# A decoder layer with 32 experts on one core: first stage, state products, output norm and first bias rearranged

## Chip, cores and metric

The kernel runs on one core of a Trainium2 chip. What is measured is device time in microseconds, the median of several runs of one program. Everything is float32. The engines are PE (TensorE, matrix products; PEld is its weight load), DVE (VectorE), ACT (ScalarE), POOL (GpSimd), SP (SyncE, which here only issues transfers) and the DMA engines. Each of the five runs its own list of instructions in order; they wait for each other by semaphores.

## The reference, cut

```python
xn = rmsnorm(h, norm1_gain[l]);  proj = xn @ w_in[l]            # h: 16 meta + 256 tokens, 1024 wide
u, q, fpre, v, og, gates = jnp.split(proj, IN_SPLITS, axis=-1)
# s5_mixer: 32 groups of 16 channels and 64 complex states each
lam_bar = jnp.exp(lam * dt)                                     # dt = exp(log_dt), one per group
b_bar = ((lam_bar - 1.0) / lam)[:, :, None] * b_mat
bu = jnp.einsum('gph,blgh->blgp', b_bar, u32)
_, states = lax.associative_scan(combine, (a, bu), axis=1)      # s_t = lam_bar * s_(t-1) + bu_t
y = jnp.real(jnp.einsum('ghp,blgp->blgh', c_mat, states)) + d_skip * u32
y = jax.nn.gelu(y);  y_s5 = y * jax.nn.sigmoid(y @ w_glu)
# hgrn2_mixer: 4 heads of 128, gated linear recurrence in chunks
o = o * lax.rsqrt(jnp.mean(o * o, axis=-1, keepdims=True) + EPS)   # the output norm, per head
y_hg = o.reshape(bsz, seq_len, HG_WIDTH) * gn_gain * jax.nn.silu(g)
merged = gate_s5 * (y_s5 @ w_branch_s5[l]) + gate_hg * (y_hg @ w_branch_hgrn[l])
h = h + merged @ w_out[l]
h = h + moe(rmsnorm(h, norm2_gain[l]), ...)   # top 4 of 32 experts: gate_up, clamped SwiGLU, down
y = rmsnorm(h, final_norm_gain)[:, N_META:]
```

The token count is 272 (16 meta tokens and 256 tokens), and only the 256 are given back. Each of the 32 experts has 8 MB of gate_up weights and 4 MB of down weights, so the expert stage reads 403 MB.

## The kernel before

**Opening.** SP loads x in two halves (xload0, xload1), the first group of w_in, then B, C and the second group of w_in. ACT's queue loads log_dt, the identity, the first gain, the eigenvalues of S5 (s5rows, three transfers into s5r and small) and the constants; POOL's queue loads the meta tokens and the small gain rows (prow, grow). DVE sums the squares of both halves (L1107), ACT takes the roots (after an Exp of log_dt, L455), DVE scales both halves (L1112), PE turns them to channels-by-tokens (L681) and DVE and ACT lay them out with the gain as xnT (L1126, L466). `keep_warm` is a run of products on ones whose result nobody reads.

**Projections.** xnT times w_in gives 36 tiles, the list PROJ: each is one bank of PSUM, made by eight products (sixteen instructions) of PE, and copied out by ACT (`next_proj`, semaphores proj and proj_free; two banks alternate). `project(n)` on PE makes the next n of the list. The first four tiles are u. Windows of w_in alternate between two places, and a window is loaded when the one before the last is used up.

**S5 constants.** DVE works out lam_bar and the factor of B on s5r, 16 partitions by 128 columns (L1120 to L1162), with Sin and Exp from ACT (L469 to L472). PE turns four rows of it (L760), DVE copies them to s5c on 128 partitions (L1167). Then the B products on DVE (L1173 to L1185), turned by PE (b_turned), laid out (b_laid), and the first product with u, `bu(0)` (L772), which also waits for the fourth tile's copy (L771).

**S5 loop.** 16 steps on DVE (L1213), each for 128 states: four products with sine and cosine, two sums, two scans, and six products back. ACT makes the sines (`turns_of`, `sines_of`), POOL moves u for the imaginary half. PE has eight rounds: LOOP_TILES says how many projection tiles stand ahead of and behind each round's `bu(p + 1)` (L780 to L785), and every second round sums the outputs (`y_of`). ACT's list of copies follows the same numbers (L526 to L554).

**HGRN2.** Seven levels (`level(n)`, PE products of 64 columns, with DVE on both sides), the glu of S5 and the other projection tiles are laid between each other by hand (L820 to L842). Behind level(5) come the state products (L836 to L840), for each of four heads one with 16 rows (the meta chunk, khTm) and one with 128 rows (khT). Then the last tiles, the outputs o (o_mm), and the branches: `branch(br, b)` makes two tiles of 256 columns of y @ w_branch. Between them stands the output norm of HGRN2: ACT squares o (o2, L592), PE sums by eight products with one column of ones (ms_mm, L871), ACT takes the root of 8 columns, DVE the reciprocal and spreads it on diagonals (dgs, L1373), PE spreads these by ones (inv_mm, L878), and DVE multiplies (yh, L1378). SP waits for inv_mm and for eight branch tiles ahead of loading pieces 3 and 4 (L359).

**Experts.** After w_out, the second norm, the router and the choice, 32 items run, one for each expert. An item's weights are six pieces of 2 MB; ten places hold pieces, and from piece 10 on SP loads piece r when r - 9 pieces are used (piece_used, L380). The first ten are loaded behind o_mm, og_used, br_mm and wo_mm (L354 to L378). An item adds the bias by four products of one-hot rows (ohb, bgu; L1021), runs four gate_up pieces, adds the item before to the sum, gathers the next item's rows, turns h, and runs two down pieces (L1006 to L1060). Ahead of item 0 the rows are gathered on PE (gather_part), copied by ACT, turned (`turn_gathered(0, 7)`, L1003) and laid by DVE. Four `keep_warm` products stand ahead of that turn (L947).

## Time and profile before

| | us |
|---|---|
| median of 3 runs (1188.56 to 1191.16) | 1188.78 |
| the profiled execution | 1189.03 |
| its span | 1187.2 |
| PE busy in it | 1152.6 |
| DVE, ACT busy | 441.7, 181.3 |

The profile's page counts 434.27 MB read from HBM, 367 GB/s over the span. The granted clock of PE has a mean of 0.994 of full speed (2.4 GHz). A row of the timeline or of a stage can cover many instructions (the x at its end); a busy PE is one that has work in flight, which is not the same as PE at its peak. An idle time in brackets says how long the engine stood before the instruction and which instruction released it.

### The profile page before, as it was taken

What the parts mean: (1) busy time and instruction counts of PE and PEld (TensorE: products, weight loads), DVE (VectorE), ACT (ScalarE), POOL (GpSimd) and SP (SyncE); (2) the same over time, 40 slices, a digit from 0 to 9 for tenths busy, and PEclk for the clock granted to TensorE, in tenths of its full rate; (3) what the DMA queues carried; (4) which work ended last, traced back from release to release, by engine and by line L of the source; (5) the groups of instructions that cost most, each with busy time, mean ns of one, the idle gap of its engine ahead of it and who ended that gap; (6) DMA issues with size and microseconds to landing.
All of it is one profiled execution on the core that took longest, in us unless ns stands there. A gap on an engine that the chain in (4) does not pass through costs nothing.

```text
span 1187.2 us, 13854 instructions
## 1 busy us (share of the span) xinstructions
PE 1152.6 (97%) x5506; PEld 501.7 (42%) x5506; DVE 441.7 (37%) x1105; ACT 181.3 (15%) x330; POOL 7.7 (1%) x19
## 2 busy tenths in 40 slices
PE   8999999999999999999999999999999999999996
PEld 7757798763333333333333333333333333333332
DVE  6889983344222222222323332222222222222224
ACT  4545732020000000000000000000000000000001
POOL 1000000000000000000000000000000000000000
...
GB/s 227 187 182 185 130 1 187 387 190 396 415 429 428 426 435 430 429 436 427 432 432 432 429 433 432 431 433 432 433 427 434 432 432 428 435 432 428 433 423 157
DMA packets 46166, 436.42 MB, mean 368 GB/s; under 512 B 17311, under 2 KB 17503, under 8 KB 30257
## 3 DMA queue, kind: packets, MB, share of 16 engines
...
q14 instruction: 10, 0.07, 0.0%
HBM read 434.27 MB, written 1.05 MB: 367 GB/s over the span
## 4 chain that ended last, share of the span: by engine, by line
PE 75%; DMA 20%; DVE 3%; ACT 1%; issue 1%; ACTq 0%; SPq 0%; DVEq 0%
PE ps L661 71%; DMA ring<-in_w_gate_up 16%; PE ps L664 4%; DMA mixed<-in_w_gate_up 3%; DVE ring L1087 1%; ACT ring L440 1%; DMA ring<-in_s_lambda_im 0%; ACT L440 0%; DVE ring L1090 0%; DVE mixed L1093 0%; DVE ring L1260 0%; DVE ring L1093 0%; ACT mixed L440 0%; DVE x L1087 0%; ACT small L440 0%
## 5 line engine op out<-in xcount | busy, mean ns | idle before, releaser
L661 PE MATMUL ps<-ring,mixed 128*64 128x512 f32 (+1 forms) x2560 | 572.0, 589 | 11.9 <-DMA ring<-in_w_gate_up 10.4
L661 PEld LDWEIGHTS ps<-ring,mixed 128*64 128x64 f32 (+1 forms) x2560 | 187.8, 139 | 356.0 <-issue 329.9
L1090 DVE TENSOR_SCALAR mixed<-ps 128x256 f32<-128x256 f32 x128 | 45.4, 417 | 585.8 <-PE ps L661 585.8
L661 PE MATMUL ps<-ring 128*128 128x256 f32 (+7 forms) x936 | 192.5, 395 | 2.5 <-DVE ring L1087 1.8
L661 PEld LDWEIGHTS ps<-ring 128*128 128x128 f32 (+2 forms) x936 | 143.9, 187 | 48.0 <-issue 26.3
L661 PE MATMUL ps<-mixed,cst 128*64 128x512 f32 (+2 forms) x776 | 160.4, 611 | 2.1 <-issue 2.1
L661 PE MATMUL ps<-mixed 128*64 128x512 f32 (+2 forms) x704 | 153.9, 561 | 2.5 <-DMA mixed<-in_w_gate_up 2.3
L440 ACT ACTIVATE mixed<-mixed 128x512 f32<-128x512 f32 (+1 forms) x36 | 24.0, 676 | 485.2 <-DVE mixed L1090 485.2
L661 PEld LDWEIGHTS ps<-mixed 128*64 128x64 f32 (+1 forms) x704 | 57.8, 144 | 87.6 <-issue 80.3
L661 PEld LDWEIGHTS ps<-mixed,cst 128*64 128x64 f32 (+2 forms) x776 | 44.9, 151 | 110.5 <-issue 110.3
L1087 DVE TENSOR_TENSOR x<-ps,x 128x512 f32<-128x512 f32 (+1 forms) x137 | 84.6, 677 | 15.1 <-PE ps L661 15.1
L440 ACT ACTIVATE mixed<-ps 128x512 f32<-128x512 f32 (+1 forms) x87 | 47.9, 553 | 269.2 <-PE ps L661 215.7
L1087 DVE TENSOR_TENSOR ring<-ring 128x256 f32<-128x256 f32 (+5 forms) x182 | 76.4, 474 | 6.6 <-PE ps L661 3.7
L664 PEld LDWEIGHTS ps<-cst,mixed 128*128 128x128 f32 x256 | 35.9, 210 | 33.5 <-DVE mixed L1087 26.2
L664 PE MATMUL ps<-cst,mixed 128*128 128x128 f32 x256 | 47.9, 310 | 1.6 <-DVE mixed L1087 1.1
L1090 DVE TENSOR_SCALAR cst<-cst,rout 128x64 f32<-128x64 f32 x192 | 44.4, 288 | 1.9 <-issue 1.8
L1562 DVE COPY mixed<-ps 128x512 f32<-128x512 f32 x32 | 22.1, 692 | 50.9 <-PE ps L664 50.9
L440 ACT ACTIVATE cst<-ps 128x256 f32<-128x256 f32 x33 | 12.7, 384 | 178.5 <-PE ps L664 178.5
L440 ACT ACTIVATE ring<-ring 128x272 f32<-128x272 f32 (+5 forms) x50 | 29.8, 602 | 10.7 <-DVE ring L1087 5.7
L1087 DVE TENSOR_TENSOR ring<-ps,ring 128x272 f32<-128x272 f32 x64 | 23.6, 428 | 3.5 <-PE ps L661 3.3
L1093 DVE SCALAR_TENSOR_TENSOR mixed<-mixed 128x512 f32<-128x512 f32 x32 | 22.2, 692 | 1.1
L1087 DVE TENSOR_TENSOR mixed<-mixed 128x512 f32<-128x512 f32 x32 | 22.1, 692 | 1.1
(145 smaller groups left out, 286.2 us busy)
## 6 DMA issues: line engine op xcount, KB each, us to landing
...
ring<-in_w_gate_up SPq DMA_DIRECT2D x28, 2048.0 KB, 16.4
ring<-in_w_down SPq DMA_DIRECT2D x20, 2048.0 KB, 22.0
...
ring<-in_w_in SPq DMA_DIRECT2D x9, 2048.0 KB, 8.8
mixed<-in_w_down SPq DMA_DIRECT2D x4, 2048.0 KB, 16.4
```

Source lines behind the costliest of these rows:

```text
L440: return nc.scalar.activation(o, i, fn, **k)
L661: return nc.tensor.matmul(o, l, r, start=start, stop=stop, skip_group_check=True)
L664: return nc.tensor.transpose(o, i, ident[0:n, 0:n])
L1087: return V.tensor_tensor(out=o, in0=i0, in1=i1, op=op)
L1090: return V.tensor_scalar(o, i, s1, s2, op0, op1) if op1 is not None else V.tensor_scalar(o, i, s1, None, op0)
L1093: return V.scalar_tensor_tensor(out=o, in0=i0, scalar=sc, in1=i1, op0=op0, op1=op1)
L1562: V.tensor_copy(hT, ps[3][:, :].rearrange("p (a b c) -> p a b c", a=4, b=2)).then_inc(s["hT_ready"], 1)
```

## The change

Five parts. **Opening:** DVE sums the squares of the first half only, ACT those of the second; each root takes mean and epsilon in one instruction, and each half is scaled and turned on its own; all of the layout is DVE's. The first two `keep_warm` runs (6 and 3 products) go, and 2 and 1 products stand behind the two turns. The three S5 rows (real, imaginary, and dt spread to the same shape) are turned ahead of the first projection, and the constants are worked out on 128 partitions by 16 columns (s5w), so no turn stands behind them. fraction(0) moves in among the B products, sines_of(0) ahead of a copy. **Tiles:** three tiles instead of four ahead of bu(0), the wait for proj_free there goes, LOOP_TILES begins with (3, 1) and ends with (2, 0), and three tiles instead of two follow the last y_of; ACT's copies move with them. **State products:** the four of 16 rows first, then the four of 128. **Output norm:** PE multiplies the squares by a full square of ones, so each partition has the sum; ACT takes the root of both 128x512 halves, DVE takes the reciprocals of both and multiplies. The branch tiles are numbered singly: one ahead of the ones products, seven behind. **First bias:** item 0's bias products stand ahead of `turn_gathered(0, 7)`, in the place of the four `keep_warm` products.

```diff
         s5r = at(ringf[0:ST], 2 * PC + 2112, 8, P)
-        s5q = at(ringf[0:ST], 2 * PC + 3136, 3, P)
+        s5w = at(ringf, 2 * PC + 3136, 9, ST)
...
-        xs = at(ringf, H0 + 4096, D)
-        xs2 = at(ringf, H0 + 5120, D)
-        v_parts = xs[:, 0:W5]
+        xsq = [at(ringf, H0 + 4096, D), at(ringf, H0 + 1536, D)]
+        xs = [at(ringf, H0 + 4096, D), at(ringf, H0 + 5120, D)]
+        v_parts = xsq[0][:, 0:W5]
...
-        LOOP_TILES = [(2, 1), (2, 1), (2, 1), (1, 2), (2, 1), (2, 1), (2, 1), (3, 0)]
+        LOOP_TILES = [(3, 1), (2, 1), (2, 1), (1, 2), (2, 1), (2, 1), (2, 1), (2, 0)]
...
-            sp.wait_ge(s["inv_mm"], 1)
+            sp.wait_ge(s["yh_ready"], 2)
             sp.wait_ge(s["br_mm"], 8)
...
-            act.wait_ge(s["s5rows"], 48)
-            f(small[0:ST, 2:4], small[0:ST, 0:2], ACT.Exp).then_inc(s["s5r_exp"], 1)
-            for t in range(TT):
-                root(1 + t, small[:, 4 + t:5 + t])
+            def mean_root(v, n):
+                return f(v, v, ACT.Sqrt, scale=1.0 / D, bias=zero_c[0:n, 2:3])
+
+            nc.scalar.preload_act_table(ACT.Sqrt)
+            act.wait_ge(s["var_in"], 1)
+            mean_root(small[:, 4:5], P).then_inc(s["root_out"], 1)
+            act.wait_ge(s["xload1"], 16)
+            link(f(xsq[1], x[:, 1, :], ACT.Square, accum_out=small[:, 5:6]))
+            mean_root(small[:, 5:6], P).then_inc(s["root_out"], 1)
             act.wait_ge(s["meta"], 16)
             link(f(xmn, xm[:, :], ACT.Square, accum_out=small[0:META, 8:9]))
-            f(small[0:META, 8:9], small[0:META, 8:9], ACT.Sqrt, scale=1.0 / D, bias=zero_c[0:META, 2:3]).then_inc(s["root_out"], 1)
-            act.wait_ge(s["inv_m"], 1)
-            f(xmn, xm[:, :], ACT.Identity, scale=small[0:META, 9:10]).then_inc(s["xm_ready"], 1)
-            act.wait_ge(s["gain1_ready"], 1)
-            act.wait_ge(s["turned_x"], TT)
-            for k in range(4, KD):
-                last = f(xnT[:, k, META + P:TOK], ps[3][:, (k - 4) * P:(k - 3) * P], ACT.Identity, scale=gain1[:, k:k + 1])
-            last.then_inc(s["xnT_ready"], 1)
+            mean_root(small[0:META, 8:9], META).then_inc(s["root_out"], 1)
+            act.wait_ge(s["s5rows"], 48)
+            f(s5r[:, 2, :].rearrange("p (g n) -> p g n", g=2), small[0:ST, 0:2].unsqueeze(2).to_broadcast([ST, 2, 64]), ACT.Exp)\
+                .then_inc(s["s5r_exp"], 1)
+            act.wait_ge(s["s5r_v"], 1)
+            f(s5c[:, 0, :], s5w[:, 3, :], ACT.Exp).then_inc(s["s5r_exp"], 1)
             act.wait_ge(s["s5r_ang"], 1)
-            f(s5r[:, 6, :], s5r[:, 5, :], ACT.Sin, scale=TWO_PI).then_inc(s["s5r_sin"], 1)
-            f(s5r[:, 7, :], s5r[:, 5, :], ACT.Sin, scale=TWO_PI / 2).then_inc(s["s5r_sin"], 1)
-            act.wait_ge(s["s5r_v"], 1)
-            f(s5r[:, 4, :], s5r[:, 2, :], ACT.Exp).then_inc(s["s5r_exp"], 1)
+            f(s5w[:, 6, :], s5c[:, 1, :], ACT.Sin, scale=TWO_PI).then_inc(s["s5r_sin"], 1)
+            f(s5w[:, 7, :], s5c[:, 1, :], ACT.Sin, scale=TWO_PI / 2).then_inc(s["s5r_sin"], 1)
...
-            next_proj(2)
+            next_proj()
             act.wait_ge(s["s5cols_ready"], 1)
             act.wait_ge(s["consts"], 16)
             turns_of(0)
             turns_of(1)
+            sines_of(0)
             next_proj()
-            sines_of(0)
...
             decay_exp(0)
-            next_proj()
+            next_proj(2)
             act.wait_ge(s["gelu_in"], 1)
             f(yt, yt, ACT.Sigmoid, scale=GELU_C).then_inc(s["gelu_sig"], 1)
...
-            act.wait_ge(s["ms_mm"], 1)
-            f(rms[:, 0:8], ps[7][:, 0:8], ACT.Sqrt, scale=1.0 / P, bias=zero_c[:, 2:3]).then_inc(s["rms_out"], 1)
+            for b in range(2):
+                act.wait_ge(s["ms_mm"], b + 1)
+                f(oms[:, 512 * b:512 * b + 512], ps[6 + b][:, :], ACT.Sqrt, scale=1.0 / P, bias=zero_c[:, 2:3])\
+                    .then_inc(s["rms_out"], 1)
...
             tr(ps[6][:, 0:8], grow1[:, :], 8).then_inc(s["gain1_turned"], 1)
-            keep_warm(6, 7)
...
-                    last = tr(ps[2 * t + k // 4][:, (k % 4) * P:(k % 4 + 1) * P], (xs, xs2)[t][:, k * P:(k + 1) * P])
+                    last = tr(ps[2 * t + k // 4][:, (k % 4) * P:(k % 4 + 1) * P], xs[t][:, k * P:(k + 1) * P])
                 last.then_inc(s["turned_x"], 1)
+                keep_warm(2 - t, 7)
             pe.wait_ge(s["xm_ready"], 1)
             for k in range(KD):
                 last = tr(ps[5][:, k * META:(k + 1) * META], xmn[:, k * P:(k + 1) * P], META)
             last.then_inc(s["turned_m"], 1)
+            pe.wait_ge(s["s5rows"], 48)
+            pe.wait_ge(s["s5r_exp"], 1)
+            for j in range(3):
+                last = tr(ps[4][:, j * ST:(j + 1) * ST], s5r[:, j, :], ST)
+            last.then_inc(s["s5rows_turned"], 1)
...
-            keep_warm(3, 7)
...
-            pe.wait_ge(s["xnT_ready"], 2)
+            pe.wait_ge(s["xnT_ready"], 1)
...
             project()
             pe.wait_ge(s["consts"], 16)
-            pe.wait_ge(s["s5r_v"], 2)
-            for j, row in enumerate((4, 5, 2, 3)):
-                last = tr(ps[7][:, j * ST:(j + 1) * ST], s5r[:, row, :], ST)
-            last.then_inc(s["s5rows_turned"], 1)
-            project()
             pe.wait_ge(s["bz_ready"], 1)
             for c in range(2):
                 for t in range(4):
@@ -768,7 +769,6 @@
             last.then_inc(s["b_turned"], 1)
             project()
             pe.wait_ge(s["b_laid"], 1)
-            pe.wait_ge(s["proj_free"], 4)
             bu(0)
             pe.wait_ge(s["s5cols_ready"], 1)
...
             y_of(ST // 4 - 1)
-            project(2)
+            project(3)
...
             for h in range(HEADS):
                 hs = slice(h * P, (h + 1) * P)
                 mm(ps[6][:, hs], khTm[:, hs], v_m[:, hs], h == 0, h == 3)
+            for h in range(HEADS):
+                hs = slice(h * P, (h + 1) * P)
                 last = mm(ps[7][:, hs], khT[:, h, :], v_a[:, 0, hs], h == 0, h == 3)
             last.then_inc(s["st_mm"], 1)
...
             pe.wait_ge(s["o2_ready"], 2)
-            for j in range(8):
-                last = mm(ps[7][:, j:j + 1], o2[:, j * P:(j + 1) * P], ones[:, 0:1], j == 0, j == 7)
-            last.then_inc(s["ms_mm"], 1)
-            branch(0, 1)
-
-            pe.wait_ge(s["diag_ready"], 1)
             for b in range(2):
-                last = mm(ps[6 + b][:, :], ones[:, :], dgs[:, 512 * b:512 * b + 512], True, True)
-            last.then_inc(s["inv_mm"], 1)
-            branch(0, 2)
-            branch(0, 3)
+                mm(ps[6 + b][:, :], ones[:, :], o2[:, 512 * b:512 * b + 512], True, True).then_inc(s["ms_mm"], 1)
+            for m in range(1, KD):
+                branch(0, m)
             pe.wait_ge(s["branchh_w"], 16)
             pe.wait_ge(s["yh_ready"], 2)
-            for b in range(4):
-                branch(1, b)
+            for m in range(KD):
+                branch(1, m)
...
             gather_part(1).then_inc(s["gathered"], 1)
-            keep_warm(4)
...
+            def add_bias(w):
+                pe.wait_ge(s["ohb_ready"], w + 1)
+                for b in range(2):
+                    for h in range(2):
+                        rows = slice(E * (2 * b + h), E * (2 * b + h + 1))
+                        last = mm(ps[b][SLOTS * h:SLOTS * (h + 1), :], ohb[rows, :], bgu[rows, :], True, False)
+                last.then_inc(s["ohb_used"], 1)
+
+            pe.wait_ge(s["expert_rows"], 64)
+            add_bias(0)
             turn_gathered(0, 7)
-            pe.wait_ge(s["expert_rows"], 64)
...
                 pe.wait_ge(s["xg_ready"], w + 1)
-                pe.wait_ge(s["ohb_ready"], w + 1)
-                for b in range(2):
-                    for h in range(2):
-                        rows = slice(E * (2 * b + h), E * (2 * b + h + 1))
-                        last = mm(ps[b][SLOTS * h:SLOTS * (h + 1), :], ohb[rows, :], bgu[rows, :], True, False)
-                last.then_inc(s["ohb_used"], 1)
+                if m > 0:
+                    add_bias(w)
...
-            for t in range(TT):
-                dve.wait_ge(s["xload%d" % t], 16)
-                link(V.tensor_tensor_reduce((xs, xs2)[t], x[:, t, :], x[:, t, :], 1.0, 0.0, MU, AD, small[:, 4 + t:5 + t]))
-                ts(small[:, 4 + t:5 + t], small[:, 4 + t:5 + t], 1.0 / D, EPS, MU, AD).then_inc(s["var_in"], 1)
-            for t in range(TT):
-                dve.wait_ge(s["root_out"], t + 1)
-                link(V.reciprocal(small[:, 6 + t:7 + t], small[:, 4 + t:5 + t]))
-                ts((xs, xs2)[t], x[:, t, :], small[:, 6 + t:7 + t], None, MU).then_inc(s["xs_ready"], 1)
+            def scaled(n, v, inv, dst, src):
+
+                dve.wait_ge(s["root_out"], n)
+                link(V.reciprocal(inv, v))
+                return ts(dst, src, inv, None, MU)
+
+            def lay_turned(t, b):
+                dve.wait_ge(s["turned_x"], t + 1)
+                tt(xnT[:, 4 * b:4 * b + 4, META + t * P:META + (t + 1) * P],
+                   ps[2 * t + b][:, :].rearrange("p (a n) -> p a n", a=4), wide(gain1[:, 4 * b:4 * b + 4], P), MU)
+
+            dve.wait_ge(s["xload0"], 16)
+            V.tensor_tensor_reduce(xsq[0], x[:, 0, :], x[:, 0, :], 1.0, 0.0, MU, AD, small[:, 4:5]).then_inc(s["var_in"], 1)
+            scaled(1, small[:, 4:5], small[:, 6:7], xs[0], x[:, 0, :]).then_inc(s["xs_ready"], 1)
             dve.wait_ge(s["gain1_turned"], 1)
             V.tensor_copy(gain1, ps[6][:, 0:8]).then_inc(s["gain1_ready"], 1)
-            dve.wait_ge(s["root_out"], 3)
-            V.reciprocal(small[0:META, 9:10], small[0:META, 8:9]).then_inc(s["inv_m"], 1)
-            R = lambda j: s5r[:, j, :]
-            R2 = lambda j: s5r[:, j, :].rearrange("p (g n) -> p g n", g=2)
-            dt2 = wide(small[0:ST, 2:4], 64)
-            dve.wait_ge(s["s5r_exp"], 1)
-            tt(R2(2), R2(0), dt2, MU).then_inc(s["s5r_v"], 1)
             dve.wait_ge(s["gain1_ready"], 1)
-            for t in range(TT):
-                dve.wait_ge(s["turned_x"], t + 1)
-                for b in range(2 - t):
-                    tt(xnT[:, 4 * b:4 * b + 4, META + t * P:META + (t + 1) * P],
-                       ps[2 * t + b][:, :].rearrange("p (a n) -> p a n", a=4), wide(gain1[:, 4 * b:4 * b + 4], P), MU)
+            scaled(2, small[:, 5:6], small[:, 7:8], xs[1], x[:, 1, :]).then_inc(s["xs_ready"], 1)
+            lay_turned(0, 0)
+            scaled(3, small[0:META, 8:9], small[0:META, 9:10], xmn, xm).then_inc(s["xm_ready"], 1)
+            lay_turned(0, 1)
+            lay_turned(1, 0)
+            lay_turned(1, 1)
             dve.wait_ge(s["turned_m"], 1)
             tt(xnT[:, :, 0:META], ps[5][:, 0:KD * META].rearrange("p (a n) -> p a n", a=KD), wide(gain1, META), MU)\
                 .then_inc(s["xnT_ready"], 1)
...
+            dve.wait_ge(s["s5rows_turned"], 1)
+            link(V.tensor_copy(s5w[:, 0:3, :], ps[4][:, 0:3 * ST].rearrange("p (a n) -> p a n", a=3)))
+            tt(real, lam_re, dt_c, MU).then_inc(s["s5r_v"], 1)
+            link(tt(angle, lam_im, dt_c, MU))
...
+            link(V.reciprocal(den_c, den_c))
             dve.wait_ge(s["s5r_exp"], 2)
             dve.wait_ge(s["s5r_sin"], 2)
...
+            link(tt(co_im, co_im, angle, SU))
+            tt(co_re, co_re, den_c, MU)
+            tt(co_im, co_im, den_c, MU).then_inc(s["s5cols_ready"], 1)
 
             dve.wait_ge(s["rows_turned"], 1)
...
             link(tt(bb[3], bim, cr, MU))
+            fraction(0)
             tt(bb[0], bb[0], bb[1], SU)
             link(tt(bb[2], bb[2], bb[3], AD))
...
-            fraction(0)
             dve.wait_ge(s["b_turned"], 1)
...
-            link(merge(0, 0))
-            dve.wait_ge(s["rms_out"], 1)
-            link(V.reciprocal(rms[:, 8:16], rms[:, 0:8]))
-            tt(dgs.rearrange("p (a n) -> p a n", a=8), wide(rms[:, 8:16], P), ident.unsqueeze(1).to_broadcast([P, 8, P]), MU)\
-                .then_inc(s["diag_ready"], 1)
+            for b in range(2):
+                root = oms[:, 512 * b:512 * b + 512]
+                dve.wait_ge(s["rms_out"], b + 1)
+                link(V.reciprocal(root, root))
+                tt(yh[:, 2 * b:2 * b + 2, :].rearrange("p a n -> p (a n)"), orn[:, 512 * b:512 * b + 512], root, MU)\
+                    .then_inc(s["yh_ready"], 1)
+            merge(0, 0)
             merge(0, 1)
-            dve.wait_ge(s["inv_mm"], 1)
-            for b in range(2):
-                tt(yh[:, 2 * b:2 * b + 2, :], orn[:, 512 * b:512 * b + 512].rearrange("p (a n) -> p a n", a=2),
-                   ps[6 + b][:, :].rearrange("p (a n) -> p a n", a=2), MU).then_inc(s["yh_ready"], 1)
```

## Rows read from the trace of the kernel before

**Rows 1.** the chain of waits in order of time: start us, us, what
```profile
145.61 95.56 PE ps L661 x468
...
799.26 36.96 DMA ring<-in_w_gate_up
...
1071.01 12.57 PE ps L661 x48
...
1129.31 10.87 PE ps L661 x48
```

**Rows 2.** busy time by stage: us, engines, PEclk, DMA share, GB/s
```profile
core 0: us, PE busy (x) PEld busy (x) DVE busy (x) ACT busy (x) POOL busy (x), PEclk, DMA share, GB/s
800.00:1000.00 200.00, 192.71 (x898) 64.08 (x896) 54.61 (x133) 14.86 (x27) 0.00 (x0) 1.00 1.00 431
```

**Rows 3.** the timeline of SP: start us, us, instruction
```profile
295.34 4.28 SPq L297 DMA_DIRECT2D mixed<-in_w_gate_up  x2
```

**Rows 4.** the same stages view as rows 2, a short stretch of item 0
```profile
294.00:296.00 2.00, 2.00 (x12) 0.54 (x8) 1.89 (x6) 0.30 (x1) 0.00 (x0) 1.00 0.18 74
```

**Rows 5.** DMA issues of the first five microseconds: KB each, us to landing
```profile
ring<-in_w_in SPq DMA_DIRECT2D x1, 2048.0 KB, 12.0
```

**Rows 6.** timeline of the first stage: start us, us, instruction [idle before it, releaser]
```profile
0.98 5.95 PE L661 MATMUL ps<-ones 128*128 128x128 f32 x28 [0.98 <-POOL ones L413]
...
11.10 1.97 PE L664 MATMUL ps<-cst,ring 128*128 128x128 f32 x16 [2.48 <-DVE ring L1090]
...
12.30 2.08 DVE L1087 TENSOR_TENSOR ring<-ps,pcol 128x512 f32<-128x512 f32 x4
...
14.64 3.83 PE L661 MATMUL ps<-ring 128*128 128x272 f32 x16
...
24.41 0.39 PE L664 MATMUL ps<-cst,ring 16*128 16x16 f32 x4 [1.44 <-DVE ring L1087]
...
28.81 1.09 PE L664 MATMUL ps<-cst,ring 128*128 128x128 f32 x8 [0.15 <-DVE ring L1090]
...
34.11 0.74 PE L661 MATMUL ps<-ring 32*128 32x272 f32 x8 [0.53 <-issue]
...
35.71 39.55 PE L661 MATMUL ps<-ring 128*128 128x272 f32 x185
```

**Rows 7.** timeline of the S5 loop and of what follows it
```profile
77.65 0.44 DVE L1093 SCALAR_TENSOR_TENSOR ring<-ring 128x272 f32<-128x272 f32 x1 [3.17 <-ACT ring L440]
...
121.30 0.38 ACT L440 ACTIVATE mixed<-ps 128x256 f32<-128x256 f32 x1 [4.94 <-PE ps L661]
...
132.75 2.97 DVE L1260 TENSOR_TENSOR_SCAN ring<-ones,ring 128x16 f32<-128x16 f32 x12 [2.47 <-ACT ring L440]
...
141.81 2.05 PE L661 MATMUL ps<-ring 128*128 128x128 f32 x16 [1.62 <-DVE ring L1087]
```

**Rows 8.** timeline of the state products, the first two pairs
```profile
177.34 0.48 PE L661 MATMUL ps<-ring,rout 16*128 16x128 f32 x2
...
177.75 0.49 PE L661 MATMUL ps<-ring 128*128 128x128 f32 x2
```

**Rows 9.** the stages view, the ten microseconds behind the state products
```profile
180.00:190.00 10.00, 10.00 (x41) 8.91 (x42) 3.27 (x8) 0.38 (x1) 0.00 (x0) 0.66 0.01 2
```

**Rows 10.** timeline of a reciprocal, and of the output norm and branches
```profile
21.03 0.94 DVE L1154 RECIPROCAL ring<-ring 16x128 f32<-16x128 f32 x1
...
198.28 1.06 ACT L440 ACTIVATE mixed<-ps 128x512 f32<-128x512 f32 x2
...
199.60 1.84 PE L661 MATMUL ps<-ones,mixed 128*128 128x1 f32 x16
...
204.84 1.88 PE L661 MATMUL ps<-ring,ones 128*128 128x512 f32 x4
...
213.47 13.98 PE L661 MATMUL ps<-mixed 128*128 128x256 f32 x64
...
213.74 0.69 DVE L1087 TENSOR_TENSOR ring<-ps,mixed 128x512 f32<-128x512 f32 x1 [2.76 <-PE ps L661]
```

**Rows 11.** timeline of item 0's bias products
```profile
267.82 0.23 PEld L661 LDWEIGHTS ps<-mixed,cst 32*64 32x64 f32 x8 [0.99 <-issue]
267.85 1.09 PE L661 MATMUL ps<-mixed,cst 32*64 32x512 f32 x8 [0.83 <-issue]
```

91 lines of the change are left out of this document (42 added, 49 removed).

## The prediction, written before the change was run

> **What bounds the kernel now.** I read the chain of waits in order of time first. Ahead of the experts its longest piece is PE alone, 95.56 us from 145.61 [rows 1]. PE also has no gap from 35.71 to 75.26, 39.55 us in one row [rows 6]; ahead of that, and from about 121 to 145, the chain goes over ACT and DVE. From 799.26 it is a transfer of expert weights that ends each step, 36.96 us at a time, with PE waiting behind it [rows 1]. The busy time by stage says the same: in 800 to 1000 the DMA engines are busy all the time (share 1.00) at 431 GB/s, and PE, 192.71 us busy of 200, is not [rows 2]. So the expert stage runs at the pace of its transfers, and the question is when their stream becomes unbroken. SP's issues tell it: piece 14 is issued at 295.34, after a wait for PE [rows 3]. In 294 to 296 the DMA share is 0.18 [rows 4]: that is the last real hole, and it ends because item 0 has used its fifth piece. From there 178 pieces follow with the queue full.
>
> So the rule of this forecast is: **every microsecond by which item 0 starts earlier moves the end by one microsecond**, and nothing inside the expert stage counts. It holds because all gates of the pieces (o_mm, br_mm, wo_mm, piece_used) are events of PE and move with it. PE's front, 0 to 268 us, is what has to be costed.
>
> **First stage.** The first projection starts at 14.64 [rows 6]. Its weights were issued at 1.64 and took 12.0 us to land, 13.64 [rows 5]; no DMA ahead of them is touched, so 13.7 is the new start if the tokens are ready by then. They are: today the first scaled half is turned at 11.10 and the tokens are complete 3.5 us later [rows 6]. Now the root of the first half waits neither for an Exp with its table nor for the second half, whose squares ACT takes beside it, so the first turns come at about 7. Behind them DVE has a second scaling, four layouts (2.08 us together [rows 6]), a small scaling and a small layout; with ACT's two squares in between I put the end at 12.3 (an estimate). Margin 1.4 us. Gain 0.9 us.
>
> Between 14.64 and the fifth tile at 35.71 PE needs 21.07 us [rows 6]. In them lie: 1.44 us of waiting for DVE ahead of the turns of the S5 rows at 24.41, the turns themselves (0.39 us, 0.3 of them not beside other work), 0.15 us ahead of the turns of B at 28.81, and 0.53 us at 34.11, where bu(0) waits for ACT's copy of the fourth tile [rows 6]. All four go: the rows are turned before the first projection, the wait for proj_free is dropped, and the fourth tile moves behind bu(0). One wait comes in. DVE can begin the B products only when the rows of prow are turned, 13.7 + 3.83 (one tile) + 0.6 = 18.15; from the end of the S5 turns (24.8) to those of B (28.81) that work took 4.0 us, and it gets 0.44 us longer by fraction(0), which is moved into it (the price of one such instruction at 77.65 [rows 7]), so the turns can start at 22.6. PE has finished its second tile at about 22.0: 0.6 us of waiting. The S5 constants on 128 partitions take some 25 short instructions of 0.15 to 0.2 us, about 5 us from 12.4, and are done before 18.15; so their own length is hidden (if it grew by more than 1 us it would show one for one). Sum: 21.07 - 1.44 - 0.3 - 0.15 - 0.53 + 0.6 = 19.25, a gain of 1.8 us. With the start, **2.7 us**.
>
> **Does it survive the S5 loop?** bu(0) is now at about 27.5 instead of 34.11, so DVE's loop starts 6.6 us earlier, but bu(1) still stands behind six tiles in all (3 + 3 for 4 + 2), and PE moves by 2.7 only. DVE will wait more in the first iterations; it had already 3.17 us of waiting at 77.65 behind ACT's share of the large v tiles [rows 7]. After that DVE runs without a gap, anchored to that point. ACT reaches the end of the loop at 121.30 after 4.94 us of waiting for PE, and DVE waits for ACT at 132.75 for 2.47 us [rows 7]. All anchors are PE's, so 2.7 us pass through. One tile is moved behind the last y_of: y_of waits for the loop's end at about 130.3 (old time) where PE used to fill in a tile. PE then idles some 2 us and finishes its tiles at 141.7 rather than 140.2; the next product waited 1.62 us for DVE until 141.81 [rows 7], so the cover is just enough. Cost taken 0, bounds 0 and 1 us.
>
> **State products by rows.** Now pairs of 16-row and 128-row products alternate, and a pair starts 0.41 us after the one before (177.34, 177.75) [rows 8]: 2.91 us for 16 instructions, 0.18 each. Sixteen 128x128 ones in a row took 2.05 us, 0.13 each [rows 7]. In two groups I take 2.05 us and one change: gain **0.8 us**; bounds 0 and 0.9.
>
> **The granted clock there.** Right behind these products the clock falls: in 180 to 190 the mean is 0.66 [rows 9], so 10 x 0.34 = 3.4 us are lost, at the lower level (1.2 GHz), in what has become the longest PE stretch of the chain. What PE did before it fell was a level product of 64 columns, the alternating pairs of 16 rows, and another level product: the thinnest seven microseconds of that stretch. Elsewhere a level product stands between full tiles. Grouping makes this thin part a microsecond shorter and takes away the alternation. I think the fall is gone more likely than not: 3.4 us, chance 0.6.
>
> The Trainium skill has a rule that speaks against the first stage (TensorE: Matmul & The Clock Gate, "HAM oscillation"): the array starts slow, activity frees it, and gaps bring it back down. The rows for it here: 28 instructions on ones took 5.95 us from 0.98, 0.21 each [rows 6], against 0.13 each for sixteen of that shape at 141.81 [rows 7]; and 2.6 us of waiting at 1071 was followed by 12.57 us for 48 products that take 10.87 otherwise [rows 1], 1.7 us lost. The change has three fillers where nine stood ahead of the first projection, and leaves PE with one short group of turns and then nothing from about 11.6 to 13.7. A gap of 2.48 us ahead of 11.10 cost nothing visible [rows 6]. I take a loss of **1.7 us** in the first tiles as likelier than none (0.6 to 0.4); bounds 0 and 3.4, the loss of rows 9.
>
> **Output norm.** PE now does in order: branch products m 0 and 1, 16 one-column products (from 199.60), m 2 and 3, two spreading products at 204.84, and m 4 to 7, until 213.47 [rows 10]. After: m 0, the ones products (as the pair at 204.84 that they replace, 1.88 us with the last drain, 1.7 without), m 1 to 7. The one-column products go, 1.84 us with their drain, 1.7 without. But m 0 ends at 196.15 + 1.73 = 197.9, and the squares come from ACT at 198.28 + 1.06 = 199.34 [rows 10], because ACT first does the gates. So 1.5 us of waiting take their place: 199.5 + 1.7 + 7 x 1.73 = 213.3 against 213.47. Gain **0.15 us**, no more. Hidden behind m 1 to 7 stands DVE's new reciprocal of 128x512, twice. 16x128 took 0.94 us [rows 10]; at that pace per column 512 take 3.8 us, so yh is ready at 201.3 + 2 x (3.8 + 0.7) = 210.3, with 3 us to spare. The merges that now wait behind it on DVE are wanted by nobody before 213. ACT's two roots from PSUM are off the path, and SP's wait on yh_ready is followed by one on br_mm that ends later.
>
> The Trainium skill says that the reciprocal is an iterated divide that repeats 8 times (VectorE: DVE Perf Modes, "First, the fixed hardware budget"). An estimate by it, 8 times the 0.69 us of a plain 128x512 (213.74) [rows 10], would be 5.5 us each and yh at 213.7: PE would wait 0.4 us. By the row it is 0.94 for 128 columns, 7.3 ns each, so 3.8 and not 5.5; I go by the row.
>
> **First bias.** The eight bias products of item 0 stood between the gathered rows and the first piece, 1.09 us from 267.85, after 0.83 us without work [rows 11]. They move to where four ones products filled the wait for ACT's copy, and these go. Nothing else is behind them: bias rows and one-hot are there long before. Gain **1.0 us**.
>
> **Sum.** 2.7 + 0.8 + 0.15 + 1.0 = 4.65 at an unchanged clock; + 3.4 for the fall that goes, - 1.7 for the first tiles: 6.35. The profiled execution took 1189.03 us (span 1187.2, and 1.8 around it), 0.25 over the median 1188.78. 1189.03 - 6.35 = 1182.7; against the median 1182.4. I say **1182.5**.
>
> **Rivals.** (a) The clock falls behind the state products as before: 2.95 with the loss in the opening, 4.65 without: 1185.8 or 1184.1. For it: the two level products stay. (b) The fall goes and the opening stays fast: 8.05, 1180.7. For it: the gap of 2.5 us that cost nothing. (c) No gain arrives: the DMA stream is set by something earlier than item 0, such as pieces 6, 8 and 9 behind wo_mm. It would give 1187 to 1189. Against it: that gate moves too, and the hole in 294 to 296. (d) Slower: DVE's reciprocals become the bound of the output norm. PE would wait for yh once each takes over 5.3 us; the total turns slower than before once each takes 8.5 us (6.4 us of gain eaten by two), 17 ns a column against 7 in the row. At 11 us each the time would be 1194. (e) It doesn't do what it says: DVE's shorter constants don't let the loop start earlier, since C or B loads come late; then only 2 us of the first part are left out, 1184.5, which is inside the range.
>
> **Chances.** Forecast (fall gone, opening slow) 0.36; (b) 0.22; (a) 0.27; (e) 0.05; (c) 0.07; (d) 0.03. Range 1180.0 to 1186.3. A difference under 0.2% (2.4 us) can't be told from none: faster 0.87, same 0.09, slower 0.04.
>
> **What would show it.** The first projection at 13.7; bu(0) near 27.5; ACT's 121.30 at 118.6 (120.3 with a slow opening); state products in about 2.1 us; the granted clock in 175 to 190 at 1.00; branch products done 13.3 us plus the stall after the last projection; item 0's first piece 4.6 to 8 us earlier than 268.87; and the same distance from there to the end. The prediction is wrong if that distance changes, if PE's first tiles are slow for more than one such stretch, or if the wait for yh shows on PE.

## The result and the profile of the changed kernel

| | before | after |
|---|---|---|
| median, us | 1188.78 (1188.47 to 1193.19, 5 runs) | 1182.27 (1181.68 to 1184.24, 5 runs) |
| profiled execution, us | 1189.03 | 1182.27 |
| its span, us | 1187.2 | 1180.4 |
| PE, DVE, ACT busy, us | 1152.6, 441.7, 181.3 | 1144.0, 443.3, 178.6 |

The ratio of the medians is 0.994, 95% interval 0.9927 to 0.9952: 6.5 us less, where 1182.5 was predicted.

The end first, as in the reading of before: the last lines of the chain of waits of the changed kernel, start, length, what it is.

```profile
792.80 38.10 DMA ring<-in_w_gate_up
...
1084.34 38.10 DMA ring<-in_w_gate_up
1122.48 10.87 PE ps L663 x48
1138.84 18.51 PE ps L663 x88
```

The row of before that answers to the last one:

```profile
1145.67 18.51 PE ps L661 x88
```

Still a transfer of expert weights ends each step from 792.80 on (799.26 in [rows 1]). PE's last 88 products start at 1138.84 instead of 1145.67, 6.83 us earlier. The span is 6.8 shorter.

SP's issues around item 0, from the timeline of the changed kernel:

```profile
252.38 1.30 SPq L296 DMA_DIRECT2D ring<-in_w_gate_up  x3
...
288.75 4.28 SPq L296 DMA_DIRECT2D mixed<-in_w_gate_up  x2
```

Piece 14 goes out at 288.75 instead of 295.34 [rows 3]: 6.59 earlier. Where these 6.59 us come from is read from front to back. PE's opening, timeline of the changed kernel:

```profile
10.47 0.91 PE L666 MATMUL ps<-cst,ring 16*128 16x16 f32 x11
13.96 5.59 PE L663 MATMUL ps<-ring 128*128 128x272 f32 x16 [2.58 <-DMA ring<-in_w_in]
...
20.12 3.93 PE L663 MATMUL ps<-ring 128*128 128x272 f32 x16
24.49 1.06 PE L666 MATMUL ps<-cst,ring 128*128 128x128 f32 x8 [0.44 <-DVE ring L1088]
```

and its stages (stretch, its length, then busy time of PE, PEld, DVE, ACT, POOL, then granted clock, DMA share, GB/s):

```profile
14.00:16.00 2.00, 2.00 (x6) 1.50 (x7) 1.73 (x13) 0.61 (x3) 0.00 (x0) 0.59 0.81 105
16.00:18.00 2.00, 2.00 (x6) 1.54 (x5) 0.85 (x8) 0.00 (x0) 0.00 (x0) 0.56 0.90 214
...
130.00:132.00 2.00, 2.00 (x9) 1.59 (x6) 0.55 (x3) 1.99 (x4) 0.00 (x0) 0.60 0.00 0
132.00:134.00 2.00, 2.00 (x7) 1.61 (x6) 2.00 (x9) 0.87 (x2) 0.00 (x0) 0.55 0.00 0
...
180.00:190.00 10.00, 10.00 (x62) 9.17 (x62) 3.11 (x7) 3.06 (x5) 0.00 (x0) 1.00 0.14 42
```

The first tile waits for its weights and runs at the lower level of the clock: 5.59 us against 3.83 for the same sixteen instructions before. The second tile is at full speed again. In 180 to 190, where before had 0.66 [rows 9], the clock is 1.00. A fall that before did not have stands in 130 to 134. The middle of the front, timeline of the changed kernel:

```profile
120.01 0.38 ACT L439 ACTIVATE mixed<-ps 128x256 f32<-128x256 f32 x1 [4.94 <-PE ps L663]
...
129.03 15.10 PE L663 MATMUL ps<-ring 128*32 128x256 f32 x80 [2.15 <-DVE ring L1085]
...
176.32 1.15 PE L663 MATMUL ps<-ring,rout 16*128 16x128 f32 x8
177.41 13.43 PE L663 MATMUL ps<-ring 128*128 128x128 f32 x88
```

ACT's copy at 121.30 [rows 7] is now at 120.01: 1.29 gained by then. PE waits 2.15 us for y_of(3), and the new fall follows. The sixteen-row state products stand together, and the group of 128 rows begins 1.09 us behind them. The end of the state products, the windows of the timeline closed where they end, first of before, then of the changed kernel:

```profile
180.25 0.62 PE L661 MATMUL ps<-ring 128*128 128x128 f32 x2
```

```profile
177.41 1.16 PE L663 MATMUL ps<-ring 128*128 128x128 f32 x8
```

A product in float32 is two instructions here. In before a row of two instructions follows every 0.41 us from 177.34 on [rows 8]: each is one of the eight products, of 16 and of 128 rows in turn, and the row at 180.25 is the eighth; the level product behind them starts at 180.66, 3.32 us from the first. In the changed kernel it starts at 178.40, 2.08 us from the first (176.32). The output norm and item 0, timeline of the changed kernel:

```profile
190.67 1.89 PE L663 MATMUL ps<-ring,mixed 128*128 128x256 f32 x8
...
193.91 1.98 PE L663 MATMUL ps<-mixed,ones 128*128 128x512 f32 x4 [1.35 <-ACT mixed L439]
...
195.73 12.25 PE L663 MATMUL ps<-ring,mixed 128*128 128x256 f32 x56
195.89 3.35 DVE L1374 RECIPROCAL ring<-ring 128x512 f32<-128x512 f32 x1 [1.20 <-ACT ring L439]
...
203.26 0.69 DVE L1085 TENSOR_TENSOR mixed<-mixed,ring 128x512 f32<-128x512 f32 x1
...
207.81 6.42 PE L663 MATMUL ps<-mixed 128*128 128x256 f32 x29
...
262.28 3.65 PE L663 MATMUL ps<-ring,mixed 128*64 128x512 f32 x16 [0.78 <-DVE mixed L1085]
```

and item 0's first piece in before:

```profile
268.87 3.65 PE L661 MATMUL ps<-ring,mixed 128*64 128x512 f32 x16
```

The S5 branch follows without a wait at 207.81, 5.66 earlier than 213.47 [rows 10]; yh was ready at 203.95. Item 0's first piece starts at 262.28, 6.59 earlier, and no bias products stand between it and the turned rows.

### The profile page after: what moved, and what is told of

The parts are those of the page before. It is cut to its first block, busy times and chain, and to the rows that moved or that the text cites. A ratio compares the mean times of both kernels' runs of the same rounds, so it can differ in the third digit from the quotient of the medians.

```text
span 1180.4 us, 13775 instructions
## 1 busy us (share of the span) xinstructions
PE 1144.0 (97%) x5469; PEld 495.1 (42%) x5469; DVE 443.3 (38%) x1103; ACT 178.6 (15%) x326; POOL 7.7 (1%) x19
## 3 DMA queue, kind: packets, MB, share of 16 engines
HBM read 434.27 MB, written 1.05 MB: 369 GB/s over the span
## 4 chain that ended last, share of the span: by engine, by line
PE 73%; DMA 20%; DVE 4%; ACT 1%; issue 1%; SPq 0%; DVEq 0%; ACTq 0%
PE ps L663 69%; DMA ring<-in_w_gate_up 16%; PE ps L666 5%; DMA mixed<-in_w_gate_up 3%; DVE ring L1085 3%; DMA ring<-in_w_in 1%; ACT mixed L439 1%; DVE ring L1231 0%; DVE ring L1233 0%; DVE mixed L1091 0%; ACT ring L439 0%; DVE ring L1088 0%; DVE mixed L1085 0%; DVE x L1085 0%; ACT L439 0%
## 5 line engine op out<-in xcount | busy, mean ns | idle before, releaser
L1085 DVE TENSOR_TENSOR ring<-ring 128x256 f32<-128x256 f32 (+5 forms) x176 | 73.9, 475 | 4.4 <-PE ps L663 4.0
L439 ACT ACTIVATE ring<-ring 128x272 f32<-128x272 f32 (+4 forms) x47 | 28.9, 621 | 6.0 <-DVE ring L1085 2.8
```

The source lines that it names most:

```text
L439: return nc.scalar.activation(o, i, fn, **k)
L1085: return V.tensor_tensor(out=o, in0=i0, in1=i1, op=op)
```

## The experiments

Theory: the end moves with the issue of piece 14, one for one; the terms are those of the prediction. Rivals: the fall of the clock is not the grouping's doing; the end is bound by something else. The changed kernel stands at 1182.27, before at 1188.65, 1189.75 and 1189.35 us beside the three sets of runs (e1 to e4, e5 to e8, the rest). "Last copy" is SP's issue of w_out, which follows ACT's copy of the last tile of projection, here in before and in the changed kernel:

```profile
192.77 0.37 SPq L352 DMA_DIRECT2D ring<-in_w_out  x1
```

```profile
187.29 0.37 SPq L351 DMA_DIRECT2D ring<-in_w_out  x1
```

**e1: only the grouping, on the kernel before.**

```diff
                 mm(ps[6][:, hs], khTm[:, hs], v_m[:, hs], h == 0, h == 3)
+            for h in range(HEADS):
+                hs = slice(h * P, (h + 1) * P)
                 last = mm(ps[7]
```

> The kernel before with one edit, the state products grouped by rows. Theory A (the alternation of 16-row and 128-row products brings the granted clock down behind it): the products take 2.1 us instead of 2.9, the stretch 180 to 190 shows a clock of 1.00, and the time is 4.4 us under before (0.8 + 0.2 + 3.4), near 1184.4. Rival B (the fall behind the state products is a matter of where in time the stretch lies, not of the order): the fall stays and the time is 1.0 us under before, near 1187.8.

Measured: 1185.90 us, ratio 0.9973 (0.9962 to 0.9984); last copy 188.22. Its stage at 180 to 190:

```profile
180.00:190.00 10.00, 10.00 (x61) 9.17 (x61) 3.19 (x8) 2.13 (x4) 0.00 (x0) 1.00 0.08 9
```

The fall is gone. The last copy is 4.55 earlier. 0.07 of it is the start of the first tile, 1.24 the products themselves (2.08 us to the next product, as in the changed kernel, instead of 3.32), and the other 3.2 is left for the clock, where its mean in 180 to 190 says 3.4. But the span (1184.1) is only 3.1 shorter, and the median lies 1.5 above theory A. That was the first sign that the end kept something. The first state product starts at 177.25, within 0.1 of before, so rival B, the place in time, is out for this execution.

**e2: the changed kernel without the grouping.** The diff of e1 undone.

> The changed kernel with the state products alternating again. Theory A: the clock falls again behind them, 3.4 us lost, and the products take 0.8 to 1.0 us longer: 4.4 us over the changed kernel, near 1186.7. Rival B: only 1.0 us over it, near 1183.3, with a clock of 1.00 there.

Measured: 1186.59 us (1182.88 to 1190.53), ratio 0.9975 (0.9959 to 0.9991). Last copy 191.33. Stages of this execution:

```profile
170.00:180.00 10.00, 10.00 (x58) 8.57 (x57) 5.90 (x10) 0.80 (x2) 0.00 (x0) 0.93 0.00 0
180.00:190.00 10.00, 10.00 (x42) 8.98 (x42) 3.11 (x7) 0.38 (x1) 0.00 (x0) 0.73 0.00 0
```

The fall is back: 0.7 + 2.7 = 3.4 us. Against the next kernel, which is the same up to there but for the grouping, the last copy is 4.6 later, 0.18 of it from a later first tile; that leaves 4.4 for products and clock, 4.5 in e1. Over all profiles: three kernels with alternating products (before, this one, e12) have the fall, eleven with grouped ones don't. The alternation is not a sure cause, though: two of the seven runs here took 1182.9 and 1183.0 us, 3.6 below the median, at a mean clock of 0.996 where the other five have 0.989 to 0.993. That would fit two executions without the fall; there is no trace of them. Nor does any run here tell the alternation from the length of the thin stretch, which the grouping shortens by 1.24 us.

**e3: the first bias and its fillers back in the old place.**

```diff
+            keep_warm(4)
...
-            add_bias(0)
             turn_gathered(0, 7)
...
-                if m > 0:
-                    add_bias(w)
+                add_bias(w)
```

> The changed kernel with item 0's bias products back behind the gathered rows and the four products on ones back in their old place. Theory A (the end moves one for one with the start of item 0): 1.0 us over the changed kernel, near 1183.3. Rival C (the stream of weights is bound by something ahead of item 0): no difference, 1182.3.

Measured: 1182.87 us, ratio 0.995 (0.9937 to 0.9963). From pieces 5 to 7 (251.83) to piece 10 (266.31) it takes 14.48 us, against 13.59 in the changed kernel: 0.89 for the bias. In the medians that is 0.6, no more than they scatter. The last copy came at 186.73, 0.56 earlier than in the changed kernel with the same order: half of it is a first tile that started 0.28 earlier, the other half that this execution had no fall at 130 to 134.

**e4: eight products on ones in the opening gap.**

```diff
             last.then_inc(s["s5rows_turned"], 1)
+            keep_warm(8, 7)
```

> The changed kernel with eight more products on ones (about 2.3 us) behind the turns of the S5 rows, where PE waits 2.58 us for the first window of w_in. Theory A (the low clock in 14.4 to 17.8 comes from the empty stretch ahead of it): the first tile takes 3.8 us instead of 5.6, the fall there is gone and the time is up to 1.7 us under the changed kernel, near 1180.6. Rival B (the place of the fall is chance and moves from run to run): no difference in the median beyond 0.5 us.

Measured: 1181.73 us (1179.73 to 1181.98), ratio 0.9931 (0.9918 to 0.9944). PE in the opening of this kernel:

```profile
11.33 2.05 PE L663 MATMUL ps<-ones 128*128 128x128 f32 x16
14.01 3.90 PE L663 MATMUL ps<-ring 128*128 128x272 f32 x16 [0.63 <-DMA ring<-in_w_in]
```

The first tile takes 3.90 instead of 5.59: the slow clock there cost 1.7, as taken. Last copy 185.37, piece 14 at 286.83, both 1.9 earlier (1.7 of it the first tile; this execution has no fall at 130 to 134 either), and the span? 1180.2 for 1180.4. The gain reaches item 0 and is lost behind it. The chain shows where: its last products come in time, 1136.93, 1.91 earlier. Then the last item, PE in the timeline, first of the changed kernel, then of this one:

```profile
1160.30 0.75 PE L666 MATMUL ps<-cst,mixed 128*128 128x128 f32 x4 [1.05 <-DVE mixed L1085]
1161.91 3.65 PE L663 MATMUL ps<-ring,mixed 128*64 128x512 f32 x16 [0.86 <-DVE mixed L1561]
```

```profile
1158.39 0.75 PE L666 MATMUL ps<-cst,mixed 128*128 128x128 f32 x4 [1.05 <-DVE mixed L1086]
1160.00 5.35 PE L663 MATMUL ps<-ring,mixed 128*64 128x512 f32 x16 [0.86 <-DVE mixed L1562]
```

The same waits of 1.05 and 0.86 us in both, for DVE; in this execution the clock has fallen behind them (0.58 in 1160 to 1162), and the sixteen products of down weights take 1.7 us more. In the items ahead of the last a transfer behind it takes up such a delay, as in [rows 1] at 1071.01. In the last there is none.

**e5 and e6: sixteen products on ones ahead of item 0's bias, and the same in item 5.**

```diff
             pe.wait_ge(s["expert_rows"], 64)
+            keep_warm(16)
             add_bias(0)
```

```diff
                 add_last(w)
+                if m == 5 and q is None:
+                    keep_warm(16)
```

> The changed kernel with sixteen products on ones (about 4.6 us on PE) ahead of item 0's bias products; they replace no wait but the 0.5 us for ACT's copy and the bias products stood in it. Theory A (the end moves one for one with item 0's start): 4.6 us over the changed kernel, near 1186.9. Rival C (the stream of weights is bound by something ahead of item 0, or has room in it): 0 to 2 us over it.

> The changed kernel with the same sixteen products on ones (about 4.6 us on PE) in the middle of item 5. Theory A (from item 0's fifth piece on the transfers set the pace, and PE gains 1.4 us an item on them): nothing, 1182.3; PE only waits less near 790. Rival D (PE's own work sets the end): 4.6 us over the changed kernel, near 1186.9.

Measured: ahead of item 0, 1187.34 us (1184.94 to 1188.83, 11 runs; the profiled one took 1185.58), ratio 0.9983 (0.9974 to 0.9992); in item 5, 1184.28 us (1181.76 to 1184.94), ratio 0.9949 (0.9935 to 0.9962). PE in the timeline of the first, then of the second:

```profile
260.37 3.84 PE L663 MATMUL ps<-ones 128*128 128x128 f32 x32
```

```profile
421.20 3.84 PE L663 MATMUL ps<-ones 128*128 128x128 f32 x32
```

The same 3.84 us: ahead of item 0, piece 14 goes out 3.6 later than in the second (293.16 for 289.52) and PE's last products start 2.8 later (1142.24 for 1139.48); the medians differ by 3.1. Inside the stage the delay leaves nothing (table below). Both had a slower opening than the changed kernel's execution (first tile 6.71 and 6.92 us for 5.59), and the second the fall in the last item, so their medians are not to be set against 1182.27 alone. The second's lies 2.0 above theory A; its profiled span is 2.3 over the changed kernel's, of which 0.8 is there at the last copy (188.06) and 1.7 is the fall in the last item.

**e7: each reciprocal of the output norm twice.**

```diff
+                link(V.reciprocal(bc[:, 0:512], root))
                 link(V.reciprocal(root, root))
```

> The changed kernel with each reciprocal of 128x512 done twice (the first time into scratch), 6.7 us more on DVE ahead of yh. Theory A (the reciprocals are hidden behind the branch products with 3.8 us to spare): yh is ready at about 210.7, PE waits for it from 207.8: 2.9 us over the changed kernel, near 1185.2. Rival E (the merges and SP's wait behind yh already cost something): the full 6.7 us, near 1189. If there were far more cover than the trace says, nothing.

Measured: 1187.02 us, ratio 0.9984 (0.9975 to 0.9993). PE at the S5 branch's first product, which was wanted at once, in this kernel:

```profile
211.17 14.05 PE L663 MATMUL ps<-mixed 128*128 128x256 f32 x64 [2.90 <-DVE mixed L1085]
```

With 6.7 us more on DVE, PE waits 2.90: there were 3.8 us of cover, 3.0 being predicted. Rival (d), reciprocals as the bound, is real as a mechanism: PE would begin to wait at 3.35 + 3.8 / 2, about 5.3 us each, as the prediction said. The median lies 1.8 above theory A and 2.0 below rival E. In the profile piece 14 goes out 3.44 later than in the changed kernel, 3.1 of it behind the last copy where 2.9 were expected, and the last item has its fall of 1.7 again.

**e8: a second branch group ahead of the ones products.**

```diff
             branch(0, 0)
+            branch(0, 1)
...
-            for m in range(1, KD):
+            for m in range(2, KD):
```

> The changed kernel with two branch tiles instead of one ahead of the ones products of the output norm, so PE's wait of 1.35 us for the squares is filled. Theory A (that wait is lost time, and yh has room behind it): 1.3 us under the changed kernel, near 1181.0. Rival F (what PE gains it waits later, for yh or for the mixers): no difference.

Measured: 1181.90 us (1181.67 to 1182.35), ratio 0.9938 (0.9925 to 0.9952). PE's wait for the squares is gone from the timeline:

```profile
190.45 3.62 PE L663 MATMUL ps<-ring,mixed 128*128 128x256 f32 x16
193.91 1.88 PE L663 MATMUL ps<-mixed,ones 128*128 128x512 f32 x4
195.62 10.52 PE L663 MATMUL ps<-ring,mixed 128*128 128x256 f32 x48
```

From the last copy (187.07) to the issue of the router's weights it is 32.92 us against 34.53: 1.6 gained. Piece 14 comes 1.8 earlier, and again the span hardly moves (1180.1), with 5.35 us for the sixteen products of the last item. So theory A holds at the front, and the median, 0.9 above it, is nearer to rival F for another reason than F's.

**e9: the moved tile put back.**

```diff
-        LOOP_TILES = [(3, 1), ..., (2, 0)]
+        LOOP_TILES = [(3, 1), ..., (3, 0)]
...
-            project(3)
+            project(2)
```

ACT's list of copies moves with it (not shown).

> The whole change, but the tile of projection that it took away behind y_of(3) is back where it was: three tiles are dealt out for the last step of the loop, and two stand ahead of the state products. The execution of the changed kernel waited 2.15 us there and had a granted clock of 0.60 and 0.55 in the two stretches of 2 us behind it; the copy of the last tile of projection ended the stage at 187.30, and other executions with the same order had no such fall and ended it at 186.7. Theory A (the missing tile opens the gap that brings the clock down, the order makes the fall likely): the wait is below 1 us, no fall at 130 to 140 in any execution, last copy at 186.6 to 186.9, median 0.4 to 1 us below that of the changed kernel (1181.3 to 1182.0). Theory B (the place of the tile is worth 0 to 1 us by itself, as my prediction bounded it, since fewer tiles stand between y_of(3) and the state products): last copy at 187.0 to 187.8, median 1182.3 to 1183. Theory C (neither): within 0.3 us of 186.73 and of 1182.3.

Measured: 1183.63 us (1181.10 to 1185.05), ratio 0.9949 (0.9936 to 0.9962); last copy 186.89. PE behind the loop in the timeline of this kernel:

```profile
126.95 11.83 PE L663 MATMUL ps<-ring 128*128 128x256 f32 x64 [0.18 <-ACT mixed L439]
140.39 2.05 PE L663 MATMUL ps<-ring 128*128 128x128 f32 x16 [1.62 <-DVE ring L1085]
...
144.19 5.51 PE L663 MATMUL ps<-ring 128*128 128x64 f32 x32 [0.16 <-DVE ring L1085]
```

level(0) stands 130.34 us behind the first tile (13.85); in e3, with the tile moved and no fall, 130.36 (144.04 and 13.68). The place of the tile is worth nothing. In the changed kernel's execution it is 130.88: the fall at 130 to 134 cost 0.5 by then, not 1.7, since a wait for DVE took the rest, and 0.3 by the first state product, 162.36 us behind the first tile for 162.08 in e3 and 162.07 here. No fall here nor in e10, the other kernel with the tile in place; with the tile moved there is one in two profiles of ten, the changed kernel's and e8's. None in two is what two in ten would mostly give too, so theory A is not shown: the missing tile may make the fall possible, but doesn't make it certain, and two waits (0.18 and 1.62 us) stay when it is back. The median lies above what all three theories said. This profile has the fall in the last item (5.23 us for the sixteen products), and the six runs spread over 4 us, so the median tells nothing on a question of 0.5.

**e12: only the opening, with its tile.** The other four parts as before.

> Of the change only the rebuilt first stage with its moved tile; the state products, the output norm and the first bias are as before. By my prediction the first stage gives 2.7 us and loses 1.7 in its two slow tiles: the copy of the last tile at 192.77 - 1.0 = 191.8 (191.5 by the 1.29 that the changed kernel had gained at the loop's fourth step), piece 14 of the first item issued at 295.34 - 1.3 = 294.0, profiled span 1186, median 1187.5, if the clock falls at 180 to 190 as in the kernel before. Rival: the fall is a matter of when the stage arrives, and an earlier opening leaves it out: last copy at 188.1, piece 14 at 290.6, span 1182.5 to 1183. Second rival: the slow opening takes all of the gain, last copy at 192.8 and median 1188.8.

Measured: 1187.39 us (1183.51 to 1191.72), ratio 0.9984 (0.9972 to 0.9995). Last copy 192.09, 0.68 earlier than before. PE in the opening of this kernel:

```profile
13.88 6.34 PE L662 MATMUL ps<-ring 128*128 128x272 f32 x16 [2.58 <-DMA ring<-in_w_in]
```

Neither rival came: the last copy is not at 188.1, though the opening is earlier, and not at 192.8, and the clock falls behind the alternating products (0.50 in 180 to 186). Here the first tile lost 2.4 us (6.34 for 3.90), not 1.7. 0.68 + 2.44 = 3.1 is what the first stage gives at full clock. Without the filler, this execution keeps a fifth of that and the changed kernel's two fifths.

**e13: both gaps of the last item filled.** On top of e4:

```diff
                 if not last_item:
                     gather(on(w + 1), 2)
+                else:
+                    keep_warm(4)
...
                 if not last_item:
                     turn_gathered(on(w + 1), 1)
+                else:
+                    keep_warm(3)
```

> The changed kernel with eight products on the constant ones while the first tile of projection waits for its weights (as in the experiment on the gap before it), and seven more in the last item of the last stage: four in the wait of 1.05 us for the vector engine's product of gate and up, three in the wait of 0.86 us for the turned values. In the profiles with a full front gain that came out too long at the end (group only, gap filled, two branches ahead) the 16 products behind these waits took 5.35 us at a clock of 0.58 instead of 3.65 at 1.00. Theory A (what the end kept of the front's gain is 1.7 us of slow clock in the last item): 3.65 us for these products in every profile, all times within 0.6 us of each other at about 1180.0, against 1181.9 and 1179.8 in two heaps without the filling. Theory B (the end is set by something else, the stream of weights or the stores of the output): the products at 3.65, and the median stays at 1181.7. Theory C (the added products delay the engine's own): median 1182 or more.

Measured: 1179.92 us (1179.85 to 1180.17, 5 runs), ratio 0.9922 (0.9909 to 0.9934). PE in the last item of this kernel:

```profile
1156.91 1.16 PE L663 MATMUL ps<-ones 128*128 128x128 f32 x8
1158.03 0.75 PE L666 MATMUL ps<-cst,mixed 128*128 128x128 f32 x4
1158.62 0.83 PE L663 MATMUL ps<-ones 128*128 128x128 f32 x6
1159.64 3.65 PE L663 MATMUL ps<-ring,mixed 128*64 128x512 f32 x16 [0.19 <-DVE mixed L1566]
```

Theory A holds: 3.65 us, 1.8 us less than e4 in the median, and all five runs within 0.32 us where e4's lay in two heaps, three at 1181.7 to 1182.0 and two at 1179.7 to 1180.0. The added products delay nothing: the sixteen start 23.06 us behind the chain's last row (1136.58), as in the changed kernel (1161.91 and 1138.84, 23.07).

**e10: all gaps filled,** that is e13 with e8's branch and e9's tile.

> The changed kernel with all gaps filled that the traces showed: eight products on the ones in the opening, the first branch's second group moved ahead of the output norm's sums, the tile back behind y_of(3), and seven products on the ones in the last item. If the end moves with the start of the first item as my prediction has it, the gains add up: opening 1.9, branch 1.6 to 1.8 (both measured at piece 14 of the first item), the tile 0 to 0.5: piece 14 at 288.75 - 3.5 to -4.2 = 284.6 to 285.3, profiled span 1176.2 to 1177.0, median 1178.0 to 1178.9, that is 0.9 to 0.991 of the kernel before at most (10 us less). Rival (the front's gain saturates, the end is bound by the stream of weights from an earlier point): median 1180 to 1181, with a longer wait or more holes in the transfers before 300.

Measured: 1178.31 us (1178.21 to 1178.34, 4 runs), ratio 0.9907 (0.9893 to 0.9921): 4.0 below the changed kernel, the fastest here. SP and the end of the chain in this kernel:

```profile
285.00 4.28 SPq L296 DMA_DIRECT2D mixed<-in_w_gate_up  x2
```

```profile
1118.61 10.87 PE ps L663 x48
1134.97 21.49 PE ps L663 x104
1158.04 3.65 PE ps L663 x16
```

Piece 14 is 1.70 earlier than in e13 and the median 1.61 lower, and piece, span (1176.5) and median all lie in the ranges written down before. Nothing saturates.

**The end, over all profiles:**

| kernel | piece 14 issued | PE's last products | distance | from there to the end |
|---|---|---|---|---|
| before | 295.34 | 1145.67 | 850.3 | 41.5 |
| after | 288.75 | 1138.84 | 850.1 | 41.6 |
| e1 | 290.79 | 1140.87 | 850.1 | 43.2 |
| e2 | 292.80 | 1143.16 | 850.4 | 41.5 |
| e3 | 289.08 | 1139.06 | 850.0 | 41.5 |
| e4 | 286.83 | 1136.93 | 850.1 | 43.3 |
| e5 | 293.16 | 1142.24 | 849.1 | 41.6 |
| e6 | 289.52 | 1139.48 | 850.0 | 43.2 |
| e7 | 292.19 | 1141.97 | 849.8 | 43.2 |
| e8 | 286.92 | 1136.85 | 849.9 | 43.2 |
| e9 | 288.35 | 1138.13 | 849.8 | 43.1 |
| e12 | 294.61 | 1144.00 | 849.4 | 41.5 |
| e13 | 286.70 | 1136.58 | 849.9 | 41.5 |
| e10 | 285.00 | 1134.97 | 850.0 | 41.5 |

Piece 14 moves over 10.3 us and the distance by 1.3, mostly within 0.3 of 850.0. The last column has two values: 41.5, and 43.1 to 43.3 where the clock falls in the last item. The fall has no order by kernel that I can see.

## Why the prediction was right

**The rule** (each microsecond of item 0 is one of the end) holds from piece 14 to the last item: 6.59 became 6.83 here, and 10.34 became 10.70 in e10. Two profiles lie off it: the distance is 849.1 in e5 and 849.4 in e12, for 849.8 to 850.4 in the others. Both issue piece 14 late, but so do before and e2, with 850.3 and 850.4; why is open.

**"The same distance to the end"** held in the execution of the changed kernel that was profiled, and failed by 1.7 us in six of the fourteen profiles. The prediction says that nothing inside the expert stage counts, and that is the step that was wrong: the last item has no transfer behind it, and its waits are not covered like those of the others. Of the changed kernel's five runs three are at 1181.7 to 1182.3 and two at 1183.8 and 1184.2. That these two are the fall in the last item would fit e4's two heaps, but there is no trace of them, and the mean clock doesn't tell it (in e4 the two short runs have 0.996, the three long ones 0.996 and 0.997). The predicted 1182.5 did not contain this term; it came out right because, as it seems, most of the runs did not either.

**First stage:** 2.7 predicted at full clock; 1.29 + 1.69 = 3.0 from the trace, 3.1 from e12. Start 13.96 for 13.7, because the weights took 12.2 us to land. The wait that comes in, ahead of the turns of B, is 0.44 for 0.6. bu(0) starts at 29.15 where 27.5 was said; it is the slow first tile, since in e4, with the gap filled, it starts at 27.52. So rival (e) is out. ACT's copy at 120.01 lies near the 120.3 named for a slow opening. **Its slow clock:** 1.7 predicted, 1.69 measured; but it is 1.4 to 3.0 in nine unfilled profiles of the new opening, and in none of them absent, so 0.6 was too low a chance for it. The Trainium skill says that a wait for a transfer can bring the array back to its slow clock (TensorE: Matmul & The Clock Gate, "HAM oscillation"). This trace agrees in direction: with the wait of 2.58 us the first tile took 5.59, with it filled to 0.63 (e4) 3.90.

**Moved tile:** 0 predicted, 0.0 measured (e9). "Cover just enough" overlooked that the clock may fall behind a wait of 2.15 us, as it did in two profiles of ten; that cost 0.3 in the profiled execution.

**State products:** 0.8 predicted, 1.24 measured (3.32 to 2.08 us), above the bound of 0.9: the term that was mis-sized most, by a misread row. The rows at 177.34 and 177.75 are the 16-row and the 128-row product of one pair, not two pairs, and the 2.91 us are 14 instructions, not 16. Each change from one kind to the other costs: in a group the instructions start 0.11 us apart, but the first one behind a change stands 0.20 from its neighbours on either side. **The fall behind them:** gone, 3.4 predicted; it is worth 3.2: from the first state product to the last copy it takes 10.97 us instead of 15.43, and 1.24 of these 4.46 are the products. e1 and e2 show it from both sides. Rivals (a) and (b) are thereby out for this execution, and (c) by e5 and e10.

**Output norm:** 0.15 predicted, 5.66 - 5.48 = 0.18 measured. The wait for the squares was 1.35 for 1.5, the reciprocals 3.35 each for 3.8. The Trainium skill states a repeat count of eight for the reciprocal (VectorE: DVE Perf Modes, "First, the fixed hardware budget"). The prediction's estimate from it, eight times a plain pass, was 5.5 and a wait of 0.4; the trace has 3.35 and no wait. Going by the row was right.

**First bias:** 1.0 predicted, 6.59 - 5.66 = 0.93 from the traces, 0.89 in e3.

**The sum** at the front is 6.59 for 6.35 predicted: 0.3 more in the opening and 0.44 more in the state products, against 0.3 for the fall at 130 to 134, 0.2 less for the clock behind the state products and 0.07 less for the first bias. The terms were off by up to 0.44 us and in part cancelled, and the five runs spread over 2.6 us, so that 1182.5 came within 0.3 of the median is in part luck.
